# One transfer for the first two weight rows, an earlier gather, and transposes one sub-block later in a decoder layer

## The reference

```python
h = rmsnorm(x, g_mix_pre[l])
proj = h @ w_in[l]
mq, mk, mv, mo, mi, mf, rq, rk, rv, rg = jnp.split(proj, SPLITS, axis=-1)
...
mix = jnp.concatenate([hm, hr], axis=-1).astype(x.dtype) @ w_out[l]
x = x + rmsnorm(mix, g_mix_post[l])

h = rmsnorm(x, g_ffn_pre[l])
ff = (jax.nn.silu(h @ w_gate[l]) * (h @ w_up[l])) @ w_down[l]
x = x + rmsnorm(ff, g_ffn_post[l])
```

## Time and profile before

| | |
|---|---|
| median of 3 runs | 1232.44 us (1231.84 to 1232.49) |
| the profiled execution | 1232.54 us |
| its span | 1230.8 us |
| TensorE busy | 1218.8 us, 99% of the span |
| VectorE busy | 715.5 us, 58% |
| ScalarE busy | 600.4 us, 49% |
| transfers | 229.49 MB, mean 186 GB/s |

### The profile page before, as it was taken

How to read it: one execution, slowest core, us unless ns; L and a number is a source line. 1 busy time by engine, 2 the same in 40 slices (tenths; PEclk the granted TensorE clock), 3 DMA queues, 4 the chain that set the end, 5 groups by cost and what they waited for, 6 DMA issues and landing times.

```text
span 1230.8 us, 15775 instructions
## 1 busy us (share of the span) xinstructions
PE 1218.8 (99%) x5899; PEld 1024.3 (83%) x5899; DVE 715.5 (58%) x919; ACT 600.4 (49%) x789; POOL 14.1 (1%) x35
## 2 busy tenths in 40 slices
PE   8999999999999999999999999999999999999997
PEld 7888888888888888888888888888888888888886
DVE  6657878877686646654555454454455454444444
ACT  5654765574655645744444444444444444343442
POOL 2000200000000000000000000000000000000000
PEclk9999999999999999999999999999999999999999
DMA  8656858668685556456565656556565665555551
GB/s 314 210 149 152 210 141 191 162 130 231 153 190 177 206 198 229 134 184 205 173 199 180 198 175 200 185 190 197 178 191 184 204 209 202 192 185 204 191 185 69
DMA packets 120553, 229.49 MB, mean 186 GB/s; under 512 B 6080, under 2 KB 22720, under 8 KB 120000
## 3 DMA queue, kind: packets, MB, share of 16 engines
q1 hardware_dynamic: 120224, 226.84, 60.7%
q0 software_dynamic: 288, 2.10, 0.4%
HBM read 226.83 MB, written 2.10 MB: 186 GB/s over the span
## 4 chain that ended last, share of the span: by engine, by line
PE 95%; DVE 2%; DMA 2%; ACT 0%; issue 0%; SPq 0%; DVEq 0%; ACTq 0%
PE bank L1288 93%; DMA raw<-in_w_in 1%; PE bank L1586 1%; DMA resid<-in_x 1%; DVE w_lo L818 1%; DVE gT L1045 0%; PE bank L1293 0%; PE bank L1502 0%; DVE h L845 0%; ACT w_hi L481 0%; DVE resid L1160 0%; PE bank L1559 0%; DVE pre L1008 0%; DVE hT L831 0%; DVE pre L1048 0%
## 5 line engine op out<-in xcount | busy, mean ns | idle before, releaser
L818 DVE TENSOR_TENSOR w_lo<-raw,w_hi 128x1024 fp32r<-128x1024 f32 x420 | 513.5, 1225 | 480.2 <-ACT w_hi L481 479.4
L481 ACT ACTIVATE w_hi<-raw 128x1024 fp32r<-128x1024 f32 x420 | 444.1, 1060 | 567.8 <-PE bank L1288 550.9
L1288 PE MATMUL bank<-w_hi,h2T 128*128 128x512 f32 x1376 | 426.6, 390 | 0.0
L1288 PEld LDWEIGHTS bank<-w_hi,h2T 128*128 128x128 f32 x1376 | 258.3, 188 | 53.2
L1288 PE MATMUL bank<-hT,w_hi 128*128 128x512 f32 x768 | 271.6, 397 | 0.0
L1288 PE MATMUL bank<-w_lo,h2T 128*128 128x512 f32 x688 | 267.7, 389 | 0.0
L1288 PE MATMUL bank<-w_hi,ffT 128*128 128x512 f32 x704 | 217.3, 389 | 0.0
L1288 PE MATMUL bank<-hT,w_lo 128*128 128x256 f32 x768 | 214.6, 279 | 0.0
L1288 PEld LDWEIGHTS bank<-hT,w_hi 128*128 128x128 f32 x768 | 144.0, 187 | 32.3
L1288 PEld LDWEIGHTS bank<-w_hi,ffT 128*128 128x128 f32 x704 | 132.2, 188 | 27.5
L1288 PEld LDWEIGHTS bank<-w_lo,h2T 128*128 128x128 f32 x688 | 129.2, 188 | 26.5
(11 more groups left out here) (173 smaller groups left out, 563.5 us busy)
## 6 DMA issues: line engine op xcount, KB each, us to landing
raw<-in_w_in SPq DMA_DIRECT2D x63, 1024.0 KB, 10.2
raw<-in_w_gate SPq DMA_DIRECT2D x44, 1024.0 KB, 5.2
raw<-in_w_up SPq DMA_DIRECT2D x44, 1024.0 KB, 5.2
raw<-in_w_down SPq DMA_DIRECT2D x44, 1024.0 KB, 5.0
raw<-in_w_out SPq DMA_DIRECT2D x16, 1024.0 KB, 5.0
resid<-in_x SPq DMA_DIRECT2D x2, 1024.0 KB, 7.1
out<-resid SPq DMA_DIRECT2D x8, 256.0 KB, 2.5
raw<-in_w_in SPq DMA_DIRECT2D x2, 512.0 KB, 6.6
```

Of the source, the lines that this page charges most:

```text
L481: act.activation(part_of(w_hi, rnd, s), src, ACT.Copy).then_inc(hi_done, 1)
L818: dve.tensor_tensor(part_of(w_lo, rnd, s), raw_sub(rnd, s)[1], part_of(w_hi, rnd, s).bitcast(F32), ALU.subtract).then_inc(lo_done, 1)
L1288: return pe.matmul(out_, lhsT, rhs, start=start, stop=stop, skip_group_check=True)
```

## The change

The first two weight rows of every partition (k tiles 0 and 1, 1 MB) come by one transfer, by the same `load` as all others. The semaphore `raw_first` is gone, and `hi` 0 waits for the whole chunk. On VectorE the first gather of the second tokens stands ahead of `lo` 1. The four blocks of transposes of tiles 8 to 15 stand behind k tiles 4, 6, 8 and 10, and the copies of them move along. The waits ahead of a block name the gathers and tiles that it needs, where they named all of them before.

```diff
--- before.py
+++ after.py
@@ -101,7 +101,7 @@
 
 def later_tiles(s):
 
-    return range(s + 5, s + 7) if s % 2 and 3 <= s < 10 else ()
+    return range(s + 4, s + 6) if s % 2 == 0 and 4 <= s <= 10 else ()
 
 
 def head_at(rnd, s, first):
@@ -265,7 +265,6 @@
         x_in = [sem(f"x_in{t}") for t in range(TT)]
         small_in = sem("small_in")
         gain_in = sem("gain_in")
-        raw_first = sem("raw_first")
         wg_in = sem("wg_in")
         post_in = sem("post_in")
         zeroed = sem("zeroed")
@@ -369,8 +368,7 @@
             sp.dma_start(resid[:, 0, :], x[0, 0:P, :]).then_inc(x_in[0], 16)
             sp.dma_start(coef[:, C_GPRE:C_GPRE + KT], g_mix_pre[0, :].rearrange("(p k) -> p k", k=KT))\
               .then_inc(gain_in, 16)
-            sp.dma_start(raw[:, 0, 0:SUB], in_rows(0, 1, 2 * DH, SUB)).then_inc(raw_first, 16)
-            sp.dma_start(raw[:, 0, SUB:2 * SUB], in_rows(1, 1, 2 * DH, SUB)).then_inc(raw_full[0], 16)
+            load(0, 0, in_rows(0, 2, 2 * DH, SUB), wait=False)
             sp.dma_start(resid[:, 1, :], x[0, P:2 * P, :]).then_inc(x_in[1], 16)
             for r in range(4):
                 for q in range(1 if r == 0 else 0, 4):
@@ -470,14 +468,11 @@
 
                 act.activation(stat[:, S_SPARE + 1:S_SPARE + 2], stat[:, S_SPARE:S_SPARE + 1], ACT.Sqrt)
 
-            def hi(rnd, s, first=False):
-
-                if first:
-                    act.wait_ge(raw_first, 16)
+            def hi(rnd, s):
+
                 rnd, s = rnd + s // 8, s % 8
                 chunk, src = raw_sub(rnd, s)
-                if not first:
-                    act.wait_ge(raw_full[chunk], 16 * (rnd + 1))
+                act.wait_ge(raw_full[chunk], 16 * (rnd + 1))
                 act.activation(part_of(w_hi, rnd, s), src, ACT.Copy).then_inc(hi_done, 1)
 
             def early_hi(s):
@@ -533,7 +528,7 @@
             act.wait_ge(gain_in, 16)
             for k in (0, 1):
                 t0_hi(k)
-            hi(0, 0, first=True)
+            hi(0, 0)
             hi(0, 1)
             for k in (2, 3):
                 t0_hi(k)
@@ -872,9 +867,9 @@
             for k in (0, 1):
                 t0_lo(k)
             lo(0, 0)
-            lo(0, 1)
             dve.wait_ge(x_in[1], 16)
             gathered(1, 0)
+            lo(0, 1)
             for k in (2, 3):
                 t0_lo(k)
             for k in (0, 1):
@@ -1432,8 +1427,8 @@
                     t1_transposed(2)
                     t1_transposed(3)
                 if later_tiles(k):
-                    pe.wait_ge(h_ready, CHUNKS * TT)
-                    pe.wait_ge(xT_lo, k + 1)
+                    pe.wait_ge(h_ready, CHUNKS + later_tiles(k)[0] // 4 + 1)
+                    pe.wait_ge(xT_lo, later_tiles(k)[1] - 8 + 1)
                     for t in range(TT):
                         transposed(h0, t, later_tiles(k)[0] // 2, first_bank)
                 if k == 11:
```

## The result

| | before | changed |
|---|---|---|
| median of 22 runs each | 1232.37 us | 1234.91 us |
| lowest to highest | 1231.77 to 1236.99 | 1233.27 to 1239.93 |
| profiled execution | 1232.54 us, span 1230.8 | 1235.16 us, span 1233.5 |

The ratio is 1.0022, 95% interval 1.0013 to 1.0031: slower by 0.2%. The interval excludes no change at all, and lies across the 0.2% at which the prediction drew its line. The time lies in the range that was given, 1.0 us above the forecast, and the executions scatter over 6 us where most of before's agree within 1 us. The scatter is the larger part of what there is to explain.

What follows compares the result with a forecast made beforehand. TensorE, busy 99% of the span, was taken as the bound. +1.02 us (k tile 1) and +0.44 us (exposed block) gave +1.46 us: 1233.9 us against the median, range 1232.0 to 1235.2 us.

Steps and rivals of the forecast that it cites:

- the 0.2% at which the prediction drew its line: Whole kernel: 0.2% (2.5 us) was taken as about what a measurement can tell from no change.
- the sum: Whole kernel: +1.02 us at k tile 1 and +0.44 us for the exposed block, +1.46 us in all.
- Landings stay: Opening transfers: weight rows still land at 9.61 us and second tokens at 12.04, despite earlier issue; chance 0.55.
- the two ends: Opening transfers: landings stay at 9.61 and 12.04 us, or come early at 8.15 and 10.58.
- The other reading: Rival, opening transfers: slow stretch goes with the half transfers, so landings come early; total 1232.4 us; chance 0.30.
- K tile 1 at 13.94: Kernel start: products of k tile 1 begin at 13.94 us in place of 12.92, +1.02 us.
- "With `lo` 1 first ... TensorE would not be sooner.": VectorE at the start: with `lo` 1 ahead, the gather would end 0.73 us later, with no gain for TensorE.
- The block behind k tile 4, +0.44: First block of four transposes leaves the wait ahead of k tile 4 and is exposed: +0.44 us.
- The clock: Rival, kernel start: 2.45 us of TensorE idleness drops its clock, adding 1.45 us, 1235.4 us total; chance 0.10.
- "It decides only if the gap of 2.45 us is enough to drop the clock": Condition for the clock rival: TensorE's idle gap from 9.62 to 12.07 us must suffice to lower its clock.
- "A start moved by some time moves the end by the same time.": From 24.51 us on, TensorE paces every engine feeding it, so a shift of the start reaches the end whole.

Runs made afterwards that it cites:

- low-clock executions: Group of executions with mean granted clock 0.997 or less within 2 us of the held ones' median: before 0 of 91; changed 7 of 34, median 1234.95 us.
- late ones: Group of executions neither held nor low-clock: before 17 of 91, median 1235.5 us; changed 10 of 34, median 1238.7 us.
- held: Group of executions with mean granted clock 0.998 or more within 1.5 us of the group's median: before 74 of 91, 1232.31 us; changed 17 of 34, 1233.82 us.
- the filled gap: Changed kernel with sixteen dummy products in place of six ahead of the first real product: median 1233.94 us, ratio 1.0013.
- the two reordered kernels: Before with the blocks moved and sub-block 4's `hi` and `lo` ahead of copies, last gathers behind; the second adds dummy products: ratios 0.9999 and 0.9993.
- the blocks alone: Before with only the four transpose blocks behind k tiles 4, 6, 8, 10 and their waits changed: ratio 1.0012.
- tokens first: Before with the second tokens' transfer issued ahead of both weight rows: one execution, 1235.67 us.
- gather only: Before with only the second tokens' first gather moved ahead of `lo` 1: ratio 1.0013.
- changed, again: The changed kernel run again without an edit: median 1234.08 us, ratio 1.0019.
- transfer only: Before with only the first two weight rows joined in one transfer, gather still behind `lo` 1: ratio 1.0017.
- before, unfilled: Before with the six dummy products ahead of the first real product removed: ratio 1.0011.

## Why the prediction came out as it did

The range held, and the sum was right for half of the executions. The missing microsecond of the median comes from a rival that I gave too small a chance, and from one thing that I took for fixed: without the low-clock executions or without the late ones the median would lie among the held.

- **Landings stay.** Right: 9.67 and 12.2 against 9.61 and 12.04. The reason was wrong. I put the slow stretch down to the gain vector's small pieces; with these moved away it stayed, and with the second tokens ahead of the weights it moved to the weights. The choice between the two ends was right by luck. The other reading, that the half transfers were slow as halves, is out too: the same 1 MB took 3.95 us as one and 3.89 as two.
- **K tile 1 at 13.94.** Measured 14.02 (clock held) and 14.10. Right, with landings up to 0.15 later.
- **"With `lo` 1 first ... TensorE would not be sooner."** Wrong. With the gather behind `lo` 1, k tile 1 came 1.78 us behind the first product, against 1.97 with the gather ahead. I had compared the ends of the gather (0.73 later; counted from the start of `lo` 0 it was 0.85), and left out that `lo` 1 is then done already, so that the product follows the transposes at once.
- **The late transfer and the early gather hide each other.** K tile 1 starts at 14.04 with the one alone, 14.01 with the other alone and 14.02 with both, against 12.92. Each alone costs all of it within 0.1 us, so undoing one part would have gained next to nothing. I worked out only the sum.
- **The block behind k tile 4, +0.44.** Right: 0.44 on the chain in the changed kernel, +0.53 in time with this part alone.
- **The clock.** The mechanism was named, and its price (1.45 us) lies between the 1.18 and 1.54 of the two profiles. Its chance, 0.10, was far off: 14 of 34 executions have a mean clock of 0.997 or less, 7 of them in the low-clock group. The trace of before showed that no gap of it dropped the clock, and I took this for evidence about longer ones. "It decides only if the gap of 2.45 us is enough to drop the clock" also asked for a yes or no where there is none: in the changed kernel the clock fell behind a gap of 2.52 us and held behind one of 2.42. Nor is it a matter of one gap: with the gather alone it fell behind three of up to 1.0 us. That idle time is the cause rests on the profiles, where the fall stands right behind the gaps, and on the filled gap, which brought eight of twelve executions to 1233.7 and left one at 0.997. The Trainium skill (TensorE: Matmul & The Clock Gate, section HAM oscillation — how this bites in real kernels) describes waits for transfers between stretches of products that drop the clock, each drop paid anew. The runs agree on the kind of cause: no execution in the low-clock group with the gap filled, 5 of 12 with the transfer alone. That a second drop is paid anew no run here shows, for none of the profiles has two while there are products left.
- **"A start moved by some time moves the end by the same time."** Not quite. The wait at 308 us isn't paced by TensorE but by loads. It was 0.5 us in before's profile, absent in the changed kernel's, and 2.0, 2.1 and 2.3 in three late ones. With the transfer alone (2.0) the clock held behind it, and the execution lies 1.9 us above the held ones; in the two reordered kernels (2.3 and 2.1) it fell, there was a wait of 0.8 or 0.9 more, and they lie 4.6 and 4.9 above. In the changed kernel's profile the start is 2.80 us late and the first product behind that wait 2.50 (310.79 against 308.29): 0.30 are given back there, and about 0.1 comes back later.

Left open: what makes those loads late in some executions, and whether the change makes it more frequent (late ones are 10 of 34 against 17 of 91 in before, which these numbers don't settle; with the blocks alone they are 6 of 12). It needn't begin with the load that lands near 305 us: with the transfer alone the chain goes back over it to one issued at 269.7 that took 19.3 us. The waits were seen in three profiles; that the other late executions have them too is inferred from their times. So are the two executions of thousands of microseconds open.

## What to carry to other kernels

In a kernel that TensorE bounds, count idle time twice: once for itself, and once for what the clock may do behind it. In the changed kernel dummy products up to the first real one cost nothing that shows (held 1233.72 against 1233.82), and with them 1 of 12 executions had a low mean clock in place of 14 of 34. Two edits that delay the same product don't add, and undoing one of them may show nothing. A transpose block that stands in a wait was free there, and cost its 0.44 us elsewhere: move the wait's cause first, and then the block. Look at how the executions are grouped before the median is explained, since a change can leave the best case as forecast and alter how often it occurs.

## What the runs showed of the hardware

- The same idle time came with either level of the clock. It fell behind gaps of 2.52 us (changed) and 2.73 (tokens first), and behind three of 0.66, 1.00 and 0.79 (gather only). It stayed at 1.00 behind 2.42 (changed, again), 2.38 (transfer only) and 1.76 (before, unfilled). Executions of one program differed: 7 of 34 of the changed kernel are in the low-clock group, and 17 are held.
- A fall cost 1.18 and 1.54 us over the eighteen products behind it, which took 4.26 at the upper level.
- The first reads of `w_in` ran at 234 to 279 GB/s for 2.5 us, by one transfer or two and with small transfers or without, where tokens in the same stretch ran at 410 (one profile).
- Issuing the second tokens' transfer 0.47 us sooner, with more than 1 MB queued ahead, made it land no sooner (12.2 against 12.04).
